# Token-shift additions of twelve projection units: from the GpSimd queue into VectorE's top-k search loop

## The reference

```python
z = u @ w_in_l                      # u = rmsnorm(h); 24 column groups of 128
zA, zB = z[..., :A_COLS], z[..., A_COLS:]
# group A: an indexer scores all keys; each query keeps its top 256 causal keys, attends over them
score = einsum('bqh,bqhs->bqs', wi, relu(einsum('bqhd,bsd->bqhs', qi, ki)))
_, idx = lax.top_k(where(causal, score, -inf), 256)
attn = softmax(q . k[idx]) @ v[idx]
# group B: the token shift, then the RWKV-7 recurrence
zB_prev = pad(zB, one row in front)[:, :T]
zB = zB + (zB_prev - zB) * mu_l     # = (1 - mu) * zB + mu * (zB of the token before)
r, k, v, xw, xa, xg = split(zB)
out = concat([attn, rwkv7(...)]) @ w_o
```

## Time and profile before

| What | Value |
|---|---|
| median of 3 runs | 4112.4 us (4112.28 to 4128.48) |
| the profiled execution | 4112.34 us, span 4110.5 us |
| PE busy | 3755.0 us, 91% of the span |
| DVE busy | 2166.3 us, 53% |
| ACT busy | 870.3 us, 21% |
| POOL busy | 555.6 us, 14% |
| shifted additions L522 | 30 on POOL, 72.7 us, mean 2424 ns |
| bit counts L1425 | 338 on DVE, 278.9 us |

### The profile page before, as it was taken

The page is one execution under the profiler, slowest core; times in us unless marked ns, Lnnn a source line. Parts: engine busy times, 40 slices in busy tenths (PEclk is TensorE's granted clock), DMA queues, the critical chain, the costliest instruction groups (busy, mean ns, idle before and its releaser), DMA issues.

```text
span 4110.5 us, 69068 instructions
## 1 busy us (share of the span) xinstructions
PE 3755.0 (91%) x29136; PEld 2851.0 (69%) x29136; DVE 2166.3 (53%) x4280; ACT 870.3 (21%) x1768; POOL 555.6 (14%) x444
## 2 busy tenths in 40 slices
PE   7999887999979999999889998869999799999995
PEld 4566555886548888888655665558865488888884
DVE  2599745666154242434646997466661642434345
ACT  1345462332010000000113446523320100000000
POOL 0041100000011222222100411000000122222220
PEclk9999997999889999999999999879998899999997
DMA  2001100000111111112210110100001111111121
GB/s 111 26 27 41 45 22 1 3 3 26 62 62 42 42 41 42 41 51 84 79 40 21 36 36 23 33 2 3 3 26 67 57 42 41 48 45 41 42 83 52
DMA packets 43384, 163.68 MB, mean 40 GB/s; under 512 B 5056, under 2 KB 5072, under 8 KB 42720
## 3 DMA queue, kind: packets, MB, share of 16 engines
q1 hardware_dynamic: 27648, 100.68, 7.2%
q0 software_dynamic: 15456, 58.85, 3.9%
HBM read 135.07 MB, written 23.49 MB: 39 GB/s over the span
## 4 chain that ended last, share of the span: by engine, by line
PE 73%; DVE 19%; issue 4%; ACT 2%; POOL 1%; DMA 0%; DVEq 0%; ACTq 0%; POOLq 0%
PE ps L712 38%; PE ps L661 9%; PE ps L742 7%; PE ps L629 6%; DVE arena L1425 4%; PE ps L903 2%; PE ps L891 2%; PE ps L916 2%; DVE little L1455 1%; PE ps L945 1%; DVE arena L1556 1%; PE ps L673 1%; PE ps L639 1%; DVE arena L1322 1%; DVE arena L1555 1%
## 5 line engine op out<-in xcount | busy, mean ns | idle before, releaser
L712 PE MATMUL ps<-arena 128*128 128x261 f32 x4096 | 924.7, 383 | 5.7 <-POOL arena L548 2.9
L712 PEld LDWEIGHTS ps<-arena 128*128 128x128 f32 x4096 | 775.1, 189 | 135.1 <-issue 5.4
L661 PE MATMUL ps<-arena,ring 128*128 128x348 f32 x2304 | 704.5, 465 | 37.1 <-DVE arena L1301 18.9
L712 PE MATMUL ps<-arena,ring 128*128 128x261 f32 x3072 | 706.4, 385 | 21.1 <-DVE arena L1778 20.7
L712 PEld LDWEIGHTS ps<-arena,ring 128*128 128x128 f32 x3072 | 585.2, 191 | 122.1 <-issue 21.2
L661 PEld LDWEIGHTS ps<-arena,ring 128*128 128x128 f32 x2304 | 439.0, 193 | 301.4 <-issue 59.6
L742 PE MATMUL ps<-arena 64*64 64x64 f32 (+1 forms) x13600 | 513.0, 226 | 97.8 <-DVE arena L1510 43.2
L742 PEld LDWEIGHTS ps<-arena 64*64 64x64 f32 x13600 | 467.6, 135 | 142.0 <-DVE arena L1556 48.8
L1280 ACT ACTIVATE aux<-ps 128x522 f32<-128x522 f32 x64 | 38.8, 607 | 1535.0 <-PE ps L712 1535.0
L1367 DVE TENSOR_TENSOR arena<-aux,ps 128x522 f32<-128x522 f32 x160 | 111.8, 699 | 423.2 <-PE ps L712 422.7
L548 POOL TENSOR_TENSOR arena<-ring 128x512 f32<-128x512 f32 x128 | 170.1, 1329 | 1106.8 <-DMA ring<-units 1101.4
(11 more groups left out here) (228 smaller groups left out, 3674.5 us busy)
## 6 DMA issues: line engine op xcount, KB each, us to landing
ring<-units SPq DMA_DIRECT2D x192, 512.0 KB, 3.7
h_scratch<-arena POOLq DMA_DIRECT2D x24, 522.0 KB, 3.1
arena<-h_scratch POOLq DMA_DIRECT2D x24, 522.0 KB, 8.3
arena<-h_in POOLq DMA_DIRECT2D x16, 522.0 KB, 9.9
out<-arena POOLq DMA_DIRECT2D x8, 522.0 KB, 3.1
arena<-att_scratch POOLq DMA_DIRECT2D x2, 2080.0 KB, 9.3
att_scratch<-arena POOLq DMA_DIRECT2D x16, 256.0 KB, 3.1
aux<-rope POOLq DMA_DIRECT2D x2, 1044.0 KB, 12.5
```

What stands on the lines that cost most here:

```text
L661: ins = mm(ps[:, b + s, 0:SW], ring[:, r * D + k * P:r * D + (k + 1) * P], tile(U0, k)[:, slice_(s)], start=(k == 0), stop=(k == KT - 1))
L712: ins = mm(acc_at(n)[:, s], lhs[:, k * P:(k + 1) * P], rhs(k)[:, s * HALF:(s + 1) * HALF], start=(k == 0), stop=(k == KT // 2 - 1))
```

## The change

GpSimd keeps the additions of units 3, 10 and 11. The twelve of units 12 to 23 move to VectorE: those of units 12 to 19 each directly ahead of the bits that ScalarE serves after that unit, those of units 20 to 23 behind the last bit and ahead of `last_step`. Each waits for `stage_in` of its unit. GpSimd waits for all additions only in layer 0, before it stores the four value tiles.

```diff
                 def add_shifted(n):
                     dst = z(ORDER[n])[:, 1:W]
-                    pool.wait_ge(S["stage_in"], w.next("stage_in"))
+                    pool.wait_ge(S["stage_in"], l * NSHIFT + shifted_before(n) + 1)
                     nc.gpsimd.tensor_tensor(dst, dst, stage[:, 0:W - 1], ALU.add).then_inc(S["z_ready"], 1)
-                    w.next("z_ready")
...
                 rope_on_pool("rot_key", key, 4)
-                for n in range(12, NZ):
-                    add_shifted(n)
-                pool.wait_ge(S["z_ready"], w.value("z_ready"))
                 if l == 0:
+                    pool.wait_ge(S["z_ready"], NSHIFT)
                     for g in range(4):
                         dma(v_dram[g], z(Z_V + g, T), "v_stored")
...
+            def add_shifted(l, n):
+
+                dst = z(ORDER[n])[:, 1:W]
+                dve.wait_ge(S["stage_in"], l * NSHIFT + shifted_before(n) + 1)
+                v.tensor_tensor(dst, dst, stage[:, 0:W - 1], ALU.add).then_inc(S["z_ready"], 1)
...
                 first_step()
-                for bit in range(BITS):
-                    bit_step(l, bit)
+                bit = 0
+                for after, bits in BITS_AFTER.items():
+                    if after in range(12, NZ):
+                        add_shifted(l, after)
+                    for bit in range(bit, bit + bits):
+                        bit_step(l, bit)
+                    bit += 1
+                for n in range(max(n for n in BITS_AFTER if n != "val") + 1, NZ):
+                    add_shifted(l, n)
                 last_step()
```

## The result

| | before | changed |
|---|---|---|
| median of runs | 4115.95 us (6 runs) | 4141.85 us (6 runs, 4136.57 to 4143.08) |
| ratio | | 1.0056, 95% interval 1.0042 to 1.0070 |
| profiled execution | 4112.34 us, span 4110.5 | 4137.18 us, span 4135.4 |

The change makes the kernel slower, by some 23 us by the ratio (25.9 by the medians of the table). Runs of the same kernel spread: 25 runs of the kernel before, taken beside the first four experiments, lay from 4111.6 to 4130.5 us around a median of 4118.9. The three runs that I had seen took in nearly all of that. Two runs of the whole record, one of the kernel before (11656 us) and one of cover_warm16 (13072 us), were slow ones and are in no ratio.

A forecast was written before the change was run, and what follows sets the result against it. VectorE's search, stalled by GpSimd's additions, was taken as the bound before 424 us. Layer 0 +12.81 - 5.85 and layer 1 +12.81 - 4.84 gave +14.9 on 4112.4: 4127.3 us, range 4116 to 4137.

The forecast's parts named there:

- Part 1: Additions 12 to 19 between VectorE's bits: stalls vanish, TensorE becomes the bound, 5.85 us gained in layer 0, 4.84 in layer 1.
- Part 2: Tail ahead of attention: last_step and the first mask lose their cover behind addition 23, costing 12.81 us a layer.
- Sum of the stage: Both layers from unit 12 to attention: +6.96 us in layer 0 and +7.97 in layer 1, together +14.9 us.
- Part 3: Attention's start: TensorE's longer idle time may move the clock's return, at most 2.5 us a layer; taken as zero.
- The additions didn't wait: Rival, additions 12 to 19 wait for stage_in or cost more, so nothing is saved: +25.6, 4138 us; chance 0.12.
- the stall was GpSimd's doing: Denies the rival that VectorE's stalls have another cause and stay, additions coming on top: over 4158 us; chance 0.02.
- Not slower: Rival, last_step and the mask find another cover in the tail ahead of attention: -13, 4099 us; chance 0.04.
- The halved duration: Rival, each of the 24 additions gives back 1.17 us by running on VectorE: -28, 4084 us; chance 0.02.
- The clock rival: At attention's start TensorE's half clock lasts 5 us longer in each layer: +5, 4132 us; chance 0.10.

The follow-up runs named there:

- cover_warm16: Changed kernel with last_step and first mask between additions 21 and 22, plus 16 extra matmuls ahead of the LoRA products: 4101.74 us, ratio 0.9964.
- cover_back: Changed kernel with last_step and the first mask moved back into the gap, between additions 21 and 22: 4117.92 us, ratio 0.9996.
- after_shift1: Changed kernel with one more 1.25 us VectorE operation ahead of the small fills, in layer 1 only: 4134.57 us, ratio 1.0046.
- before_warm: Kernel before with 33 extra matmuls, results never read, on TensorE ahead of the LoRA products in both layers: 4129.18 us.
- cover_pin: Changed kernel with last_step and first mask between additions 21 and 22, plus extra matmuls ahead of and among the LoRA products: 4096.25 us, ratio 0.9921.
- adds_12_19: Kernel before with only additions 12 to 19 moved to VectorE, 20 to 23 staying on GpSimd: 4105.1 us, ratio 0.9969.
- before_pin: Kernel before with extra matmuls, 16 ahead of the LoRA products and more among them and the first head sums: 4124.48 us, ratio 0.9988.

## Why the prediction was wrong

Forecast 4127.3 us within 4116 to 4137; measured 4141.85. Slower was the right direction, the size was not.

- *Part 1, additions 12 to 19: right.* The stall is gone, the addition doesn't wait. An addition costs the search 303.37 - 302.21 = 1.16 us, not 1.28, as the next instruction starts before it ends. TensorE became the bound. From unit 12's start to unit 23's end the gain is 177.7 - 170.4 = 7.3 and 175.8 - 170.4 = 5.4 us, where I had 5.85 and 4.84. I had added the lengths of three pieces, and each row's length runs on 0.27 us past where the next piece can start (28.35 us against 96 starts 0.2925 us apart). That is 0.5 us a layer. In layer 0 the profile before also ran unit 12 at half clock until 281.6, 5.3 us from its start; the changed one did so for 4.1 us, until 283.1. That is another 1 us, and luck of the clock.
- *Part 2, the tail: right to 0.1 us.* 19.19 - 6.35 = 12.84 and 19.07 - 6.35 = 12.72 us against 12.81.
- *Sum of the stage:* +12.9 against +14.9, off by part 1's sizes.
- *Part 3 is the step that failed,* with the last sentence of the sum, that "attention and all behind it hang on `attn_in` and move along". I weighed TensorE's clock at attention's start only, and took zero. There it is right within 1.1 us in both layers. But the LoRA stage, 160 us further on, has no fixed length: 86.6 or 96.4 us in layer 1, 63.6 or 72.2 in layer 0, by where the granted clock falls. The changed kernel had the long one in layer 1 in both its profiles, +9.9 us. To this its first profile adds 2.7 us ahead of unit 12, its second the long one of layer 0, +8.6 us.
- *What I could have seen:* and the page's clock row show half clock in such stages, and the three runs before spread over 16 us, more than the effect I forecast. A range for a kernel like this has to carry the excesses of every stage at mixed clock, some 9 us each, and not the clock of one.
- *The rivals.* The additions didn't wait, and the stall was GpSimd's doing, as both are seen directly. "Not slower" needed another cover for the tail; cover_back shows that order alone makes it in the stage (15.1 us less than before), though its median is that of before. The halved duration isn't the gain: the eight between the bits gave what TensorE's idle time was. The clock rival was right in kind, wrong in place.

Open: what ends the full clock after 6.8 us in one run and after 17.1 us in another. The time of the stage's start may matter: all four runs of after_shift1, whose records start 0.5 us later, lie under the lowest of the changed kernel, but there is one profile of it. The idle time ahead doesn't explain it, since before_warm, with the 11 us filled and no wait over 2.8 us ahead of its fall in layer 1, fell too. The Trainium skill (TensorE: Matmul & The Clock Gate, section What's actually happening) says that the activity window runs free of the kernel's start, so that the number of slow matmuls at the start of the same kernel differs from run to run. The two profiles of the kernel before differ in such a way, 63.6 and 72.2 us for the same stage; that this is the cause here, in the middle of a kernel, is argued, not shown. And that the excess sits in layer 1 of the changed kernel more often than in the one before rests on two profiles each and the medians.

## What to carry to other kernels

An instruction that moves to another queue takes its wait along: ask what stands behind it there. Here four additions of 1.25 us cost 12.8 us a layer, as 14 us of work that had been done in a gap came behind the last of them; the other eight, moved alone, gained 13 us, and the best versions keep the gain and the gap. The ratios are 0.9921 for cover_pin, 0.9964 for cover_warm16 and 0.9969 for adds_12_19, which has no extra matmuls; each is to the kernel before in its own round, with medians of 4130.1, 4112.2 and 4118.9 us, so by the times themselves (4096.3, 4101.7, 4105.1 us) they lie closer. Read a stall on the engine that suffers it: GpSimd had 1% of the chain and cost VectorE 2.15 us an addition. And where TensorE changes its clock in stages that aren't touched, compare kernels stretch by stretch before believing a difference of 10 us.

## What the runs showed of the hardware

- A VectorE operation on 7 columns (0.23 us) that starts while GpSimd runs a two-input addition takes until that ends (L1455 up to 2.39 us). The counts L1425, with one tensor input, run beside it at their usual length (0.61 us at 384 columns, beside it or alone). One tensor input alone doesn't make it so: L1466 has one and took 2.28 in place of 0.17 us. The Trainium skill (SBUF — State Buffer, section Who interferes with whom) calls this an exclusive lock on a port pair that both share; the rows agree, 405.79 + 2.37 = 408.16 us against GpSimd's 408.14.
- TensorE's granted clock falls to half while it is fully busy: 14.00 us of 14, clock 0.59, in before_pin, with products of 32 rows and a matmul of 128 rows behind each three. The same products, 48 records, take 18.3 or 27.3 us in kernels that do the same just ahead of them.
- A float32 matmul is two records in the trace: 33 of 348 columns are "x66" and take 19.57 us. So a unit, 8 weight tiles times 3 slices, is 24 matmuls in 48 records, where the description of the kernel has 48 matmuls, and the 48 records of the LoRA products, called 48 matmuls in the expectations, are 24.
- A 1.25 us VectorE addition is followed by the next instruction after 1.16 us.
